# Two-layer RWKV-7 trunk on eight cores: the recurrence step written as a 64-wide transition matrix and an offset

## The reference, cut to what matters

```
S_t = S_{t-1} (diag(w_t) + a_t^T b_t) + v_t^T k_t ;  y_t = S_t r_t
```

## Time and profile before

| what | value |
|---|---|
| median of 3 runs (lowest, highest) | 5159.62 us (5111.48, 5221.91) |
| the profiled execution | 5108.12 us, span 5106.6 us |
| cores in it | 5056.2 to 5106.6 us, granted clock 0.916 to 0.922 |
| PE, DVE, ACT, POOL busy | 79%, 52%, 31%, 15% of the span |
| sections of layer 0, first to last chunk chain | about 381 to 1841 us |
| sections of layer 1 | about 3350 to 4640 us |

### The profile page before, as it was taken

One profiled execution on the slowest core, in us unless ns is written; L12 is line 12 of the kernel. 1 busy time (PEld: TensorE's weight loads), 2 busy tenths in 40 slices (PEclk: granted clock), 3 DMA queues, 4 the chain that ended last, 5 costly groups with the idle time before them and its releaser, 6 DMA issues.

```text
span 5106.6 us, 100622 instructions; the slowest of 8 cores (5056.2 to 5106.6 us)
## 1 busy us (share of the span) xinstructions
PE 4029.8 (79%) x37524; PEld 1963.2 (38%) x37524; DVE 2670.0 (52%) x6207; ACT 1576.6 (31%) x3172; POOL 755.5 (15%) x1025
## 2 busy tenths in 40 slices
PE   1159998998998976666748888589988889888688
PEld 1124444444444432333323333244444444444333
DVE  1347777777777730000005556367667776672054
ACT  0234444443443410000000033245444444442101
POOL 1011001011001023333320000210111011102210
PEclk9999999999998987888879999799989899999899
DMA  9432123122123047777785723431323133316993
GB/s 162 103 40 29 23 36 38 21 34 34 22 28 37 20 56 80 87 85 84 85 128 126 143 100 116 79 39 27 38 35 43 19 39 44 45 22 77 132 162 139
DMA packets 634334, 339.03 MB, mean 66 GB/s; under 512 B 491616, under 2 KB 616832, under 8 KB 625408
## 3 DMA queue, kind: packets, MB, share of 16 engines
q0 software_dynamic: 532752, 170.85, 32.5%
q1 hardware_dynamic: 101104, 161.74, 9.9%
HBM read 431.96 MB, written 71.32 MB: 99 GB/s over the span
## 4 chain that ended last, share of the span: by engine, by line
PE 57%; DVE 14%; issue 9%; DMA 9%; ACT 5%; POOL 2%; SPq 2%; DVEq 1%; ACTq 0%; POOLq 0%
PE pb L396 40%; PE pBU L396 7%; DVE big L425 6%; ACT big L409 5%; PE pF L396 5%; DVE big L413 4%; DMA big<-w_in 4%; PE pBY L396 2%; PE pFC L396 2%; DMA big<-w_ada 2%; POOL big L141 2%; DMA big<-sgT 2%; SPq L141 2%; PE pFC L400 1%; DVE big L417 1%
## 5 line engine op out<-in xcount | busy, mean ns | idle before, releaser
L396 PE MATMUL pb<-big 128*128 128x512 bf16 (+4 forms) x10656 | 2686.9, 391 | 479.9 <-DMA big<-w_in 330.8
L396 PEld LDWEIGHTS pb<-big 128*128 128x128 bf16 (+3 forms) x10656 | 952.4, 101 | 1574.8 <-issue 729.7
L141 POOL DMA_DIRECT2D big<-w_in x648 | 482.3, 771 | 2973.8 <-PE pb L396 2186.9
L409 ACT ACTIVATE big<-pb 128x512 f32<-128x512 f32 (+1 forms) x456 | 220.6, 486 | 1506.3 <-PE pb L396 1427.7
L396 PE MATMUL pF<-big 64*64 64x64 bf16 (+2 forms) x11240 | 584.0, 225 | 90.5 <-DVE big L413 67.1
L421 DVE TENSOR_SCALAR big<-big 128x512 bf16<-128x512 f32 (+3 forms) x352 | 134.9, 383 | 840.0 <-ACT big L409 830.5
L413 DVE TENSOR_TENSOR big<-big 128x512 bf16<-128x512 f32 (+8 forms) x800 | 462.6, 580 | 77.9 <-ACT big L409 35.0
L396 PEld LDWEIGHTS pF<-big 64*64 64x64 bf16 (+1 forms) x11240 | 350.3, 109 | 336.7 <-issue 215.0
L409 ACT ACTIVATE big<-pFC 128x512 bf16<-128x512 f32 (+1 forms) x655 | 389.3, 594 | 260.8 <-PE pFC L396 201.2
L396 PE MATMUL pBU<-big 64*64 64x64 bf16 (+2 forms) x2560 | 362.0, 220 | 128.5 <-DVE big L425 63.5
L409 ACT ACTIVATE big<-big 128x512 bf16<-128x512 f32 (+4 forms) x472 | 321.2, 692 | 391.9 <-DVE big L413 193.6
(11 more groups left out here) (118 smaller groups left out, 2558.1 us busy)
## 6 DMA issues: line engine op xcount, KB each, us to landing
big<-w_in POOLq DMA_DIRECT2D x648, 128.0 KB, 4.7
big<-x SPq DMA_DIRECT2D x32, 1024.0 KB, 6.9
big<-w_ada POOLq DMA_DIRECT2D x256, 128.0 KB, 5.6
sgT<-big SPq DMA_DIRECT2D x192, 128.0 KB, 2.1
big<-sgT SPq DMA_DIRECT2D x192, 128.0 KB, 4.1
big<-w_ada POOLq DMA_DIRECT2D x32, 512.0 KB, 36.2
big<-w_out POOLq DMA_DIRECT2D x32, 512.0 KB, 26.5
xmid<-big SPq DMA_DIRECT2D x16, 1024.0 KB, 4.7
```

The lines of the kernel that those rows point to most:

```text
L141: return e.dma_start(out=out, in_=in_)
L396: self.P.op("pe", lambda e: e.matmul(rv(out), lhsT, rhs, start=start, stop=stop), r, w, cost=max(140.0, self._n(out) * mult) / 2400.0)
L409: return e.activation(out=rv(out), in_=rv(in_), func=func, scale=scale, **kw)
```

## The change

The state of a chunk is now updated by a matrix that is made ahead of time: H' = W (D^T H + H + O), where `DT` (64x64 per chunk and head) and the offset `OW` are made in `sF` for all chunks at once. y is made from a corrected `r` (`rt4`, in place in `ar[:, 1, :]`), so that its state-free part is done in `sF` and its state part for all 8 chunks after the chain. `G`, `Ub`, `Hb`, `wcp` go, `Hall` keeps all 8 states of a section. Only the sequential part and the end of `sF` change; `sP`, `sD` and their weight loads keep their code.

```diff
@@ sF, from the last round of the doubling on
-                k.cp(d_["mX"], FCu, ["pbFC"], ["mX" + sk], eng="act")
-                for (h, c) in u2:
-                    k.mm(fb[hds(h), (c // 2) * 64:(c // 2) * 64 + 64], a_tok[hv, c // 2, h * 64:(h + 1) * 64],
-                         d_["mP"][hv, u, :], True, True, ["a_tok", "mP" + sk], [FKEYS[c % 2]])
-                k.cp(d_["atp"].rearrange(...), pF.rearrange(...), FKEYS, ["atp" + sk], eng="dve")
+                k.cp(XA[:, :, 0, :], FCu, ["pbFC"], ["XAx"], eng="act")
+                for (h, c) in u2:
+                    k.mm(Fu[hv, u, :], mP[hv, u, :], XA[hv, u, :, :], True, True, ["mP", "XAx", "XAa"], [FKEYS[h]])
+                k.cp(ZA[:, :, 0, :], Fu[:, :, 0:64], FKEYS, ["ZAz"], eng="act")
+                k.cp(ZA[:, :, 1, :], Fu[:, :, 64:128], FKEYS, ["ZAa"], eng="dve")
+                for (h, c) in units:
+                    k.mm(o_, kt_tok[hv, b, hc], v_tok[hv, b, hc], True, False, ...)
+                    k.mm(o_, bt_tok[hv, b, hc], ZA[hv, u, 0, :], False, True, ...)
+                    k.mm(Fp[hds(h), c % 2, b, 64:128], ZA[hv, u, 1, :], bt_tok[hv, b, hc], True, True, ...)
+                k.cp(d_["DT"]..., Fp[:, :, :, 64:128], FKEYS, ["DT" + sk], eng="act")
+                k.tt(d_["OW"]..., Fp[:, :, :, 0:64], Wt...[:, :, :, 64:65].to_broadcast([128, 2, 4, 64]), ALU.mult, ...)
+                if full:
+                    for (h, c) in units:
+                        k.mm(Fp[hds(h), c % 2, b, 0:64], ZA[hv, u, 1, :], mRB[hv, u, :], True, True, ...)
+                    k.tt(rt4, Fp[:, :, :, 0:64], rt4, ALU.add, FKEYS + ["ar" + sk], ["rtp" + sk])
+                    if si > 0:
+                        P.ctl("need", "By%d" % (si - 1))
+                    for par in range(2):
+                        for b in range(4):
+                            for h in range(2):
+                                k.mm(o_, v_tok[hv, b, hc], mRK[hv, u, :], first and b == 0, False, ..., ["pbY"])
+                                k.mm(o_, ZA[hv, u, 0, :], mRB[hv, u, :], False, False, ..., ["pbY", ...])
                 P.ctl("mark", "F2%d" % si)
@@ sB_, one section
                 P.ctl("need", "F2%d" % si)
+                k.stt(HOW, Hn, Wt[:, 0, 64:65], OW[:, 0, :], ALU.mult, ALU.add, ...)
                 for c in range(8):
-                    k.mm(BU[hv, 0:128], atp[:, c * 64:(c + 1) * 64], Ho, True, False, ...)
-                    for h in range(2):
-                        k.mm(BU[hv, h * 64:(h + 1) * 64], mP[hv, un(h, c), :], mX[hv, un(h, c), :], False, h == 1, ...)
-                    k.cp(Ub[hv, :], BU[hv, 0:128], ["pbU"], ["Ub%d" % (c % 2)], eng="act")
-                    if full:
-                        k.mm(BY[:, c * 64:(c + 1) * 64], Ho, ar[:, 1, c * 64:(c + 1) * 64], True, False, ...)
                         for h in range(2):
-                            k.mm(BY[...], vtk[...], mRK[...], False, False, ...)
-                    k.mm(BU[:, 128:256], ktt[hv, b, :], vtk[hv, b, :], True, False, ...)
-                    k.mm(BU[:, 128:256], btt[hv, b, :], Ub[hv, :], False, True, ...)
-                    if full:
-                        for h in range(2):
-                            k.mm(BY[...], Ub[...], mRB[...], False, True, ...)
-                    k.stt(G, G, wc_prev, BU[:, 128:256], ALU.mult, ALU.add, ...)
-                    k.stt(Hn, G, Wt[:, c, 64:65], bd1, ALU.mult, ALU.mult, ...)
+                        k.mm(BU[hds(h), 0:64], DT[hds(h), c, :], Hall[hds(h), c, :], True, True, ...)
+                    k.stt(Hn, BU[:, 0:64], Wt[:, c, 64:65], HOW, ALU.mult, ALU.add, ...)
+                    if c < 7:
+                        k.cp(Hall[:, c + 1, :], Hn, ["Hn"], ["Ha%d" % (c + 1) + sk], eng="act")
+                        k.stt(HOW, Hn, Wt[:, c + 1, 64:65], OW[:, c + 1, :], ALU.mult, ALU.add, ...)
+                if full:
+                    for c in range(8):
+                        for h in range(2):
+                            k.mm(BY[hds(h), c * 64:(c + 1) * 64], Hall[hds(h), c, :], ar[hds(h), 1, c * 64:(c + 1) * 64], False, c == 7, ...)
                     k.cp(f_y, BY, ["pbY"], ["f_y"], eng="act")
+                    P.ctl("mark", "By%d" % si)
```

More of the change, by code:

```diff
@@ L706, in main_phase @@
             d_["z2"] = A.take([128, W], F32)
[L707 to L712, removed]
+            d_["DT"] = A.take([128, 8, 64], BF16)
+            d_["OW"] = A.take([128, 8, 64], F32)
+            d_["Hall"] = A.take([128, 8, 64], BF16)
             ST.append(d_)
@@ L716, in main_phase @@
         vb = A.take([128, W], BF16)
-        a_tok = A.take([128, 4, 128], BF16)
+        kt_tok = A.take([128, 4, 128], BF16)
+        bt_tok = A.take([128, 4, 128], BF16)
+        v_tok = A.take([128, 4, 128], BF16)
+        mRB, mRK, mP = (A.take([128, 8, 64], BF16) for _ in range(3))
+        XA = A.take([128, 8, 128], BF16).rearrange("p u (a t) -> p u a t", a=2)
+        ZA = A.take([128, 8, 128], BF16).rearrange("p u (a t) -> p u a t", a=2)
         NP = [A.take([128, 8, 128], BF16).rearrange("p u (a t) -> p u a t", a=2) for _ in range(2)]
@@ L723, in main_phase @@
         yo = [A.take([128, W], BF16) for _ in range(2)]
-        Ub = A.take([128, 128], BF16)
-        G = A.take([128, 128], F32)
-        Hb = [A.take([128, 128], BF16) for _ in range(2)]
+        Hn = A.take([128, 64], F32)
+        HOW = A.take([128, 64], F32)
         vt = A.take([128, 3, 8], F32)
@@ new lines, in sF @@
+                Wt = d_["Wt"]
+                k.cp(d_["DT"].rearrange("p (b a) x -> p a b x", a=2), Fp[:, :, :, 64:128], FKEYS, ["DT" + sk], eng="act")
+                k.tt(d_["OW"].rearrange("p (b a) x -> p a b x", a=2), Fp[:, :, :, 0:64],
+                     Wt.rearrange("p (b a) x -> p a b x", a=2)[:, :, :, 64:65].to_broadcast([128, 2, 4, 64]), ALU.mult,
+                     FKEYS + ["Wt" + sk], ["OW" + sk])
+                if full:
+                    for (h, c) in units:
+                        u, hv, b = un(h, c), halfs(c), c // 2
+                        k.mm(Fp[hds(h), c % 2, b, 0:64], ZA[hv, u, 1, :], mRB[hv, u, :], True, True, ["ZAa", "mRB"], [FKEYS[c % 2]])
+                    rt4 = ar[:, 1, :].rearrange("p (b a t) -> p a b t", a=2, t=64)
+                    k.tt(rt4, Fp[:, :, :, 0:64], rt4, ALU.add, FKEYS + ["ar" + sk], ["rtp" + sk])
+                    if si > 0:
+                        P.ctl("need", "By%d" % (si - 1))
+                    for par in range(2):
+                        first = par == 0
+                        for b in range(4):
+                            c = 2 * b + par
+                            for h in range(2):
+                                u, hv = un(h, c), halfs(c)
+                                hc = slice(h * 64, (h + 1) * 64)
+                                o_ = BY[hds(h), c * 64:(c + 1) * 64]
+                                k.mm(o_, v_tok[hv, b, hc], mRK[hv, u, :], first and b == 0, False,
+                                     ["v_tok", "mRK"] + ([] if first else ["PE:ye"]), ["pbY"])
+                                k.mm(o_, ZA[hv, u, 0, :], mRB[hv, u, :], False, False,
+                                     ["ZAz", "mRB"], ["pbY", "PE:ye" if first else "PE:yo"])
```

84 lines of the change are left out of this document (41 added, 43 removed).

## The result

| | before | after |
|---|---|---|
| median of 4 runs | 5135.55 us | 4984.26 us |
| profiled execution | 5108.12 us | 4861.39 us |
| section period, layer 0 / layer 1 | 46.4 / 40.9 us | 43.2 / 36.6 us |
| eight chunks, first to last | 22.8 us | 11.3 us |

The ratio is 0.9535, with a 95% interval of 0.9424 to 0.9646: 4.7% faster. The medians hold executions in which one half of the chip was granted less clock; the ratio and all that follows leave those out, which is why 4984 stands beside a profile of 4861. The forecast was 4916 us in 4790 to 5090, faster with 0.71.

A forecast was written before the change was run, and what follows sets the result against it. It took PE's own time, filled with projections, to bound the sections. From 5108 us it took 206 us of relief (four fifths of 258) and added 14 us net for moved matmuls: 4916 us, range 4790 to 5090 us.

The forecast's parts named there:

- 206 us of relief: Sections of both layers: the part of PE's 258 us relief from the new chunk form that the time was to show.
- 29 us of moved matmuls: Sections: 134 large matmuls now stand behind the last layer norm, relieving the sections of 29 us, all counted.
- The tails: Behind the sections: 77 moved matmuls add 31 us in layer 0, 57 add 12 us in layer 1.
- What a chunk takes from PE: Full section: PE's cost of small matmuls and shape changes falls from 9.7 to 5.3 us; half section, 6.6 to 3.65.
- the four fifths: Sections: share of PE's 258 us relief that the time sees, taken between all and half: 206 us.
- DVE and ACT: Per section: DVE net -0.3 us of 34, ACT +1.0 us on 20; DVE busy 81% at 42 us a section.
- What bounds the kernel: Sections with the recurrence, 2731 of 5107 us: PE is filled with projections; chunks cost PE's own time.
- the state never comes late: Section start: chunks begin 0.14 us after `sF`'s last operation ended, so `sP`, `sE` and `sF` set the pace.
- All of it, and waits too: Rival, chance 0.12: sections give all 258 us, and PE's waits before `pBU`, 116 us, vanish: 4748 us.
- Half of it: Rival, chance 0.23: the order's table overprices small matmuls, PE waits for `pF` evictions, half the relief is lost: 4993 us.
- The end of `sF` sets the pace: Rival, chance 0.12, slower: new `sF` links add 3.7 us per full section, 1.8 per half: 5328 us, or 5225.
- The clock: Rival, chance 0.08: the denser order is granted 0.85 of PE's clock throughout, costing 200 us: 5110 us.

## Why the prediction was right, and where it was not

**Size and sign: right; both parts came out better than due.** Of the sections, 206 us of relief and 29 us of moved matmuls, 235 us, were due. Between the lines shown they measured 234.5, but those are 62 of the 64 periods and two different cores. By the means of all cores, 32 x 3.46 + 32 x 4.49 = 254 us. The tails were to give back 43 us and gave back about 6. Both errors go the same way; with the start, 6 us longer, they make up the 50 us by which the mean of the cores gained more than the forecast's 192 us (55 by the slowest cores).

**What a chunk takes from PE, 9.7 against 5.3 us: borne out in layer 0.** PE's busy time per section fell by 5.0 us, where 4.4 and half a microsecond of moved matmuls were due. The pair took 0.15 to 0.22 us. The bursts were not priced one by one, and a busy time also holds what the clock does.

**How it divides: the four fifths were a mean of two wrong halves.** A section of layer 0 gained 3.2 to 3.7 us, where four fifths of 4.4 and 0.6 for moved matmuls, 4.1, were due. Layer 1, half of it half sections, gained 4.5 us (2.9 and 0.4 due), more than the whole of PE's price, 3.7 and 0.4. There the granted clock had risen from 0.92 to 0.94, which on 36 us of busy time is 0.8 us by my estimate; no run separates it from the rest.

**DVE and ACT: right.** 0.280 and 0.256 us for 64 columns where 0.25 and about 0.24 were taken; DVE's time per section did not move. Its share rose to 77%, not to the 80% named.

**The tails: wrong.** 31 us were due behind layer 0 and 12 behind layer 1; measured were -4 and -14 on the cores shown, +6 and -7 by the mean of all. Part of it is where the stretch starts: it holds the last section's chunk chain, 11.3 us shorter. From the last section's first chunk to the first gate stored took 20.0 us before and 30.7 after, so from the end of the chunk chain the first gate comes 22 us later, which is the moved work; but the 32 gate items then ran at 24.0 us each and not 24.6. They are not touched by the change: in another core of the same execution of before that same stretch took 1498 us and not 1530. The term of 31 us is no larger than what this stretch varies by from core to core.

**What bounds the kernel: half right, and the number owes something to luck.** "PE is filled, and what the chunk costs is PE's own time" holds in layer 0 of the kernel before: 3.46 us more of PE cost 3.5. But taking 7 us away gave 1.1, and in layer 1 nothing, while the change gave 4.5 there. So below the filled PE the runs without filler show a second bound, at about 45 us in layer 0, and by them a relief of PE alone would have been stopped there. The change lowered that one too, to 41.7, and nothing in the prediction says why. It is not the layer norm's place in the reuse of the buffers, and in the changed kernel not the length of the chunk chain. What it is stays open. The lower clock without filler is one candidate; the old chunk chain, twice as long, is another for the kernel before. A third is the loop through `sE` and `sF`: from `sF`'s first eviction to the first chunk it now takes 36.6 us of a period of 42.9. The sentence "the state never comes late" had that sign in it: chunks that start as soon as `sF` ends are chunks that wait for `sF`. The run that would show it, the program's order replayed with one stream's waits removed at a time, was not made.

**Rivals.** "All of it, and waits too": PE's waits before `pBU` did not vanish, 69.0 us became 69.9 in layer 0. "Half of it" named a real fault, the price of a small matmul in the order's table, but not what it does: the sections gave at least their 235 us, and the 69 us of the other price came from filler set into PE's gaps. One other price was tried, once, so how much of that is the better price and how much another order by chance is not shown. "The end of `sF` sets the pace" did not happen as a slowdown, though PE's wait for `pF` behind DVE rose from 1.1 to 1.5 us a section and `sF` grew from 28.1 to 36.6 us from its first eviction to the first chunk. "The clock" stayed above 0.9: 0.94 in both stretches.

## What to carry to other kernels

Cost a small matmul by what it does to the engine around it: three changes of shape per chunk took a third of a microsecond from the large ones, on top of 0.89 us for ten small ones; bursts of 16 took 0.25 to 0.42 us. Before you say that an engine is the bound, both add work to it and take work away, and look at the clock in each run; here the two answers differed. Read a period together with how much filler stands in it. And where a cost table writes the order, try its prices against the trace: one price was worth 69 us beside 242 for the whole rewrite. A stretch in which one engine waits for weights beside a stretch with idle DMA was worth 170 us more.

## What was not expected of the hardware

Less work made PE slower: without the filler the sections were granted 0.87 (before) and 0.89 (after) of the clock instead of 0.97 and 0.96, with PE busy 84% and 77% of the time, and PE gave back in slower matmuls about 3 and 2 of the 7 us removed (an estimate: 34 and 32 large matmuls at 0.216 us, less the fall of the busy time per section). All cores of these executions agree to 0.02. In layer 1 of the kernel before it was 0.77 with PE busy 81%. In the changed kernel with its filler the engine was busy 86% and the clock stayed at 0.94 to 0.96. The busy share alone does not tell the clock: with the modulation vectors inside the sections PE was busy 87% of layer 0's and was granted 0.91.
